# Four gate pairs as 7-product Strassen between the query and the pooling units, attention with one filler unit per block, three pooling groups on GpSimd

## The reference

```
h = RMSNorm(x) * (1 + scale1(c)) + shift1(c)          # from c @ w_ada (1024 x 6144)
u, q, k, v, ga, gb = split(h @ w_in)                  # widths 512, 512, 128, 128, 1024, 1024
A = pool(u) @ w_a      # 4 groups of 128: causal mean over 2, 4, 8, 16 tokens minus token, 128 x 128 map, scale
B = attention(q, k, v) @ w_b     # window 128, 8 heads on 2 kv heads, ALiBi, sinks
x = x + gate1(c) * ((sigmoid(ga) * A + sigmoid(gb) * B) @ w_out)
h2 = RMSNorm(x) * (1 + scale2(c)) + shift2(c)
x = x + gate2(c) * (relu(h2 @ w_up)^2 @ w_down);  y = RMSNorm(x)
```

## Time and profile before

| | |
|---|---|
| median of 3 runs | 1286.92 us (1286.79 to 1288.46) |
| the profiled execution | 1287.11 us, span 1285.4 us |
| TensorE matmul / weight load busy | 1264.3 us (98%) / 1237.8 us (96%) |
| VectorE, ScalarE, GpSimd busy | 826.5 (64%), 557.2 (43%), 191.2 us (15%) |
| moved by DMA | 211.59 MB, mean 165 GB/s |

### The profile page before, as it was taken

One profiled execution on the slowest core, in us unless ns is written; L12 is line 12 of the kernel. 1 busy time (PEld: TensorE's weight loads), 2 busy tenths in 40 slices (PEclk: granted clock), 3 DMA queues, 4 the chain that ended last, 5 costly groups with the idle time before them and its releaser, 6 DMA issues. The chain is left out here.

```text
span 1285.4 us, 24641 instructions
## 1 busy us (share of the span) xinstructions
PE 1264.3 (98%) x10165; PEld 1237.8 (96%) x10165; DVE 826.5 (64%) x1264; ACT 557.2 (43%) x969; POOL 191.2 (15%) x183
## 2 busy tenths in 40 slices
PE   6999999999999999999999999999999999999997
...
PEclk9999999999999999999999999999999999999999
...
GB/s 324 311 313 277 135 67 68 70 90 75 67 68 76 201 150 70 172 119 148 123 115 189 164 162 135 143 166 127 167 333 271 216 196 209 216 248 195 181 126 102
DMA packets 238556, 211.59 MB, mean 165 GB/s; under 512 B 17169, under 2 KB 219797, under 8 KB 233565
## 3 DMA queue, kind: packets, MB, share of 16 engines
...
...
## 5 line engine op out<-in xcount | busy, mean ns | idle before, releaser
L603 PE MATMUL psum<-xh,b_lo 128*128 128x264 f32 x908 | 257.8, 284 | 0.0
L601 PE MATMUL psum<-xh,b_hi 128*128 128x264 f32 x908 | 256.7, 283 | 0.0
L602 PE MATMUL psum<-xl,b_hi 128*128 128x264 f32 x908 | 256.2, 282 | 0.0
L601 PE MATMUL psum<-dh,e_hi 128*128 128x264 f32 x896 | 255.0, 285 | 0.0
L602 PE MATMUL psum<-dl,e_hi 128*128 128x264 f32 x896 | 253.9, 283 | 0.0
L603 PE MATMUL psum<-dh,e_lo 128*128 128x264 f32 x896 | 253.7, 283 | 0.0
L601 PE MATMUL psum<-h_hi,w_hi 128*128 128x384 f32 (+1 forms) x624 | 207.9, 333 | 3.0 <-issue 1.7
L602 PE MATMUL psum<-h_lo,w_hi 128*128 128x384 f32 (+1 forms) x624 | 201.5, 323 | 0.0
L603 PE MATMUL psum<-h_hi,w_lo 128*128 128x384 f32 (+1 forms) x624 | 201.3, 323 | 0.0
L602 PEld LDWEIGHTS psum<-xl,b_hi 128*128 128x128 f32 x908 | 170.5, 188 | 0.0
L601 PEld LDWEIGHTS psum<-xh,b_hi 128*128 128x128 f32 x908 | 170.5, 188 | 0.0
(11 more groups left out here) (320 smaller groups left out, 2359.0 us busy)
## 6 DMA issues: line engine op xcount, KB each, us to landing
...
```

What stands on the lines that cost most here:

```text
L601: mm(out, whi, rhi, start=first, stop=False)
L602: mm(out, whi, rlo, start=False, stop=False)
L603: return mm(out, wlo, rhi, start=False, stop=last)
```

## The change

Four of the eight gate pairs leave the attention blocks. They become 28 Strassen products (`gp`), 7 for each pair, between z units 5 and 6: T1 to T4 of h are made during units 2 to 5 (`tx_dve`, `tx_high`, at the tiles in `TX_DVE`, `TX_ACT`), weights come in blocks of 512 rows (`load_gp`), VectorE adds the products up (`gp_product`) and each half gate goes to DRAM by itself (`keep_gate`). The w_ada products move up to before tile 9, the sample attention to tiles 12 to 20; its inputs load during the last pair. An attention block keeps one filler unit: z unit 9 in the first, then gate units. Scores, parting and weighing of neighbouring blocks interleave otherwise, in other banks. Pooling groups 1 to 3 are computed on GpSimd, in blocks 0 to 3, behind its casts. Elsewhere only semaphore counts shift. Cut to its core, eight columns of indentation less:

```diff
 Z_ROW = (KZ, VZ, 0, 1, 2, 3, 4, 5, 6, 7)
-N_Z, N_G, N_AB, N_O = 10, 16, 8, 16
+PAIRS = 4
+N_GP = 7 * PAIRS
+N_Z, N_G, N_AB, N_O = 10, 2 * (DK - PAIRS), 8, 16
...
+TX = [(x, tok) for x in (T1, T2, T3, T4) for tok in range(2)]
+N_T = len(TX)
+TX_DVE = {0: (("raw", T1, 0),), 1: (("raw", T1, 1),), 2: (("raw", T2, 0),), 3: (("raw", T2, 1),), 4: (("low", T1, 0), ("low", T1, 1)),
+  7: (("low", T2, 0), ("low", T2, 1)), 10: (("raw", T3, 0), ("raw", T3, 1), ("raw", T4, 0), ("raw", T4, 1)),
+  11: (("low", T3, 0), ("low", T3, 1))}
+TX_ACT = {2: ((T1, 0),), 3: ((T1, 1),), 5: ((T2, 0),), 6: ((T2, 1),), 11: ((T3, 0), (T3, 1))}
+def gp_place(j, w):
+    return {"11": 0, "21": 1, "12": 3, "22": 2 + 2 * (j % 2)}[w]
...
+GP_BASE = [16 * sum(gp_place(*r) == k for r in GP_LOADS) for k in range(6)]
+def gp_sum(n):
...
...
-REST_SLOT = (0, 1, 0, 1, 0, 1, 1, 1)
-REST_AT = {1: 0, 3: 1, 5: 2, 7: 3, 9: 4, 12: 5, 15: 6, 18: 7}
+REST_SLOT = (0, 1, 0, 1, 0, 1, 0, 1)
+REST_AT = {0: 1, 2: 2, 3: 3, 5: 4, 6: 5, 8: 6, 9: 7}
...
...
@@ -708,11 +788,17 @@
                     last.then_inc(ready[3 * s + t], 1)
                 if (k, s, t) in ((1, 0, 0), (2, 1, 0), (4, 0, 0)):
                     pair_turn({1: 1, 2: 2, 4: 3}[k])
+                if (k, s, t) == (6, 1, 2):
+                    rest_rows(0)
+                if (k, s, t) == (7, 0, 1):
+                    rest_turn(0)
...
+    for u in range(2, N_Q):
         for t in range(3):
             i = 3 * (u - 2) + t
             if i - 1 in REST_AT:
                 rest_turn(REST_AT[i - 1])
             if i in REST_AT:
                 rest_rows(REST_AT[i])
...
+    for n in range(N_GP):
+        i, bank = n % 7, 2 * (n % 4)
+        wait(pe, free[bank], take(bank, ("gp", n)))
+        if n < 4:
+            wait(pe, free[bank + 1], banks.n[bank + 1])
+        pe.wait_ge(b_lo_done, n + 1)
...
+            for k in range(4):
+                last = mm3(psum[:, bank + tok, 0:HB], gp_hi[n % 3][:, k, :], gp_lo[n % 3][:, k, :], xhi[:, k, :], xlo[:, k, :], k == 0, k == 3)
+        last.then_inc(ready[bank], 1)
+    copied(("gp", N_GP - 4))
+    for u in range(N_Q, N_Z - 1):
+        for t in range(3):
+            i = 3 * (u - 2) + t
...
+            if t == 0:
+                pe.wait_ge(w_lo_done, u + 1)
+            tile(("z", u, t), t, t, u, h_hi, h_lo)
+    copied(("gp", N_GP - 1))
...
     for i in range(BLK):
-        u = W_G + 2 * i
-        turn_values(i)
+        kind, u = FILL[i]
         scores(i)
         pe.wait_ge(w_lo_done, u + 1)
-        tile(("g", u, 0), 0, 0, u, h_hi, h_lo)
-        tile(("g", u, 1), 1, 1, u, h_hi, h_lo)
-        tile(("g", u, 2), 2, 2, u, h_hi, h_lo)
-        turn_probs(i, 0)
+        tile((kind, u, 0), 3 * i % 2, 0, u, h_hi, h_lo)
+        if i:
+            weigh(i - 1)
+        turn_values(i)
+        tile((kind, u, 1), (3 * i + 1) % 2, 1, u, h_hi, h_lo)
         if 1 <= i < 5:
             pool_map(i - 1)
-        pe.wait_ge(w_lo_done, u + 2)
-        if i == BLK - 1:
-            last_gate(i, u + 1)
-            continue
-        tile(("g", u + 1, 0), 0, 0, u + 1, h_hi, h_lo)
-        turn_probs(i, 1)
-        tile(("g", u + 1, 1), 1, 1, u + 1, h_hi, h_lo)
-        weigh(i)
-        tile(("g", u + 1, 2), 2, 2, u + 1, h_hi, h_lo)
-        if i == 5:
+        if i == 6:
             pe.wait_ge(tail_done, 1)
             wait(pe, free[3], take(3, "pool_last"))
             for g in range(NG):
@@ -876,6 +972,12 @@
             for g in range(NG):
                 last = nc.tensor.transpose(psum[0:NB * PAD, 4, g * P:(g + 1) * P], pool_tail[:, g, :], ident[:, :])
             last.then_inc(ready[4], 1)
+        tile((kind, u, 2), 3 * i % 2, 2, u, h_hi, h_lo)
+        turn_probs(i, 0)
+        if i < BLK - 1:
+            turn_probs(i, 1)
+    pe.wait_ge(w_lo_done, W_G + N_G)
+    last_gate(BLK - 1, W_G + N_G - 1)
...
+    def tx_high(x, tok):
+        act.wait_ge(n2_t, TX.index((x, tok)) + 1)
+        if x == T2:
+            for j in range(4, DK):
+                act.wait_ge(xt_saved[j], 16)
+        fn(tx_hi[x, tok][:, :, :], tx_raw[x, tok][:, :, :], ACT.Copy).then_inc(n2_hi, 1)
+    def gp_high(n):
...
+        act.wait_ge(landed_sem, value)
+        there(last_of[4] if n == 0 else last_of[5] if n < 3 else ("gp", n - 3))
+        fn(gp_hi[n % 3][:, :, :], place[:, :, :], ACT.Copy, scale=-1.0 if n % 7 == 6 else 1.0).then_inc(b_hi_done, 1)
...
+    for u in range(2, N_Q):
+        if u + 1 < N_Q:
+            split_hi(u + 1)
+        else:
+            gp_high(0)
...
-            if i == 12:
+            for what in TX_ACT.get(i, ()):
+                tx_high(*what)
+            z_copy(u, t)
+    for n in range(N_GP):
+        j, i = divmod(n, 7)
+        if n == 0:
+            gp_high(1)
+        if n + 2 < N_GP:
+            gp_high(n + 2)
+        if n < 2:
+            tx_high(T4, n)
+        if i < 2:
+            done = there(("gp", n))
...
+            bank, _ = turn["gp", n]
+            fn((gp_m1, gp_m5)[i][:, :, :], psum[:, bank:bank + 2, 0:HB], ACT.Copy).then_inc(done, 1)
+    split_hi(N_Q)
...
-        u = W_G + 2 * i
+        u = FILL[i][1]
         split_hi(u + 1)
+        if u + 1 == W_P:
+            split_hi(W_G)
+        fill_copy(i, 0)
+        exps(i, 0)
+        if i:
+            o_copy(i - 1)
         done = there(("v", i))
         fn(v_tok[:, i % 2, :], psum[:, 7, 0:P], ACT.Copy).then_inc(done, 1)
-        exps(i, 0)
-        gate_copy(i, 0, 0)
         exps(i, 1)
-        gate_copy(i, 0, 1)
-        gate_copy(i, 0, 2)
+        fill_copy(i, 1)
...
+        fill_copy(i, 2)
+    split_hi(W_AB)
...
@@ -1578,6 +1734,7 @@
         if p < 3:
             by_token(2 * p + 3)
     split_lo(2)
+    rest_add(0)
...
+    def tx_dve(what, x, tok):
+        raw = tx_raw[x, tok][:, :, :]
+        if what == "low":
+            dve.wait_ge(n2_hi, TX.index((x, tok)) + 1)
...
+            tt(tx_lo[x, tok][:, :, :], raw, f(tx_hi[x, tok][:, :, :]), ALU.subtract).then_inc(h2_done, 1)
+            return
+        if x == T1:
+            ch.step(tt(scr[tok][:, :, :], f(half_x(h_hi, X12, tok)), f(half_x(h_lo, X12, tok)), ALU.add))
+            ch.step(tt(raw, scr[tok][:, :, :], f(half_x(h_hi, X11, tok)), ALU.subtract))
+            tt(raw, raw, f(half_x(h_lo, X11, tok)), ALU.subtract).then_inc(n2_t, 1)
+        elif x == T2:
+            ch.step(tt(raw, f(half_x(h_hi, X22, tok)), f(half_x(h_lo, X22, tok)), ALU.add))
+            dve.wait_ge(n2_t, TX.index((T1, tok)) + 1)
+            tt(raw, raw, tx_raw[T1, tok][:, :, :], ALU.subtract).then_inc(n2_t, 1)
+        else:
+            dve.wait_ge(n2_t, TX.index((T2, tok)) + 1)
+            y = X11 if x == T3 else X21
+            ch.step(tt(raw, scr[tok][:, :, :], f(half_x(h_hi, y, tok)), ALU.subtract))
+            tt(raw, raw, f(half_x(h_lo, y, tok)), ALU.subtract).then_inc(n2_t, 1)
...
+    def gp_low(n):
+        dve.wait_ge(b_hi_done, n + 1)
+        place, hi, lo = gp_from(n)[0][:, :, :], f(gp_hi[n % 3][:, :, :]), gp_lo[n % 3][:, :, :]
+        if n % 7 == 6:
+            stt(lo, place, -1.0, hi, ALU.mult, ALU.subtract).then_inc(b_lo_done, 1)
+        else:
+            tt(lo, place, hi, ALU.subtract).then_inc(b_lo_done, 1)
+    def gp_product(n):
+        j, i = divmod(n, 7)
+        if i < 2:
+            return
+        done = there(("gp", n))
+        bank, turns = turn["gp", n]
...
+        if i == 2:
+            freed(("gp", n - 2))
+            tt(u, p, m1, ALU.add).then_inc(done, 1)
+            dve.wait_ge(done, turns + 1)
+            freed(("gp", n - 1))
+            wait(dve, g_saved[0], 32 * j)
+            ch.step(tt(c12, u, m5, ALU.add))
+        if i == 3:
+            tt(c12, p, c12, ALU.add).then_inc(done, 1)
+        if i == 4:
+            tt(u, p, u, ALU.add).then_inc(done, 1)
+            dve.wait_ge(done, turns + 1)
+            wait(dve, g_saved[1], 32 * j)
+            tt(c22, u, m5, ALU.add).then_inc(c_done, 1)
+        if i == 5:
+            tt(c11, p, m1, ALU.add).then_inc(done, 1)
+        if i == 6:
+            tt(c21, p, u, ALU.add).then_inc(done, 1)
...
-    for u in range(2, N_Z):
+    dve.wait_ge(h_done, DK)
+    dve.wait_ge(hs_done, DK // 2)
+    for u in range(2, N_Q):
         for t in range(3):
             i = 3 * (u - 2) + t
             if i - 1 in REST_AT:
                 rest_add(REST_AT[i - 1])
-            if i == 12:
+            if t == 0 and u + 1 < N_Q:
+                split_lo(u + 1)
+            if t == 0 and u + 1 == N_Q:
+                gp_low(0)
+                gp_add(1)
+                gp_add(2)
+            for what in TX_DVE.get(i, ()):
+                tx_dve(*what)
+    for n in range(N_GP):
+        if n == 0:
+            gp_low(1)
+        else:
+            gp_product(n - 1)
+        if n + 2 < N_GP:
+            gp_low(n + 2)
+        if n + 3 < N_GP and gp_sum(n + 3):
+            gp_add(n + 3)
+        if n < 2:
+            tx_dve("low", T4, n)
+    gp_product(N_GP - 1)
+    split_lo(N_Q)
...
+            if i in S_NORM:
```

(147 more changed lines are left out.)

249 lines of the change are left out of this document (158 added, 91 removed).

## The result

The changed kernel takes **1302.29 us** (median of 4 runs, 1301.51 to 1306.33) against 1287.03; the ratio is 1.0123, 95% interval 1.0101 to 1.0145, so it is slower by 15.3 us. The forecast was 1290.6 with a range of 1281 to 1300: the side was right, the size was not, and the time lies 2.3 us above the range.

The account below looks back on a forecast made before the run. TensorE's work, plus any waits put into it, was taken to bound the kernel: span 1285.4 - 12.2 + 9.4 + 3.0 + 0.5 + 3.0 = 1289.1 us, forecast 1290.6 against the median, range 1281 to 1300.

Parts of the forecast that it names:

- Products: Four gate pairs as seven products each, 120.5 ns per matmul: 3.04 us saved per pair, 12.2 us in all.
- The w_ada loads: Eight 2 MB blocks, needed earlier while DMA engines are full, stall TensorE 9.4 us; bounds 5.8 to 12.9.
- Rest 1: w_ada block needed before tile 0: lands at 65.8 us, stalling TensorE 2.75 us.
- Rest 3: w_ada block needed before tile 3: queued behind other loads, lands at 84.0 us, stall 2.5 us.
- Rest 6: w_ada block needed before tile 8: queued behind gate blocks, leaves at 105.2 us, stall 3.9 us.
- T3 and T4: VectorE derives them at tile 10, 13.4 us against TensorE's 10.4, so product 1 is late by 3.0 us.
- Behind the last product: VectorE drains it, then splits unit 6, while TensorE has 1.5 us of turning: 0.5 us wait.
- Attention: Blocks with one filler: GpSimd's pooling sums and VectorE stop one another, 3 us reach TensorE; bounds 0 and 14.
- (a): Rival: w_ada loads stay mostly hidden, DMA engines moving 400 GB/s in the mix, a gain, say 1283 us; chance 0.25.
- (b): Rival: GpSimd and VectorE starve one another in attention blocks 1 to 3, up to 14 us: 1302; chance 0.14.
- (c): Rival: gate products miss the feed-forward pace, at 125 ns per matmul the saving falls by 3 us: 1294; chance 0.09.
- rival (d): New TensorE stalls drop the clock to 1.2 GHz for 4 us of work behind each: 1300 us; chance 0.05.

Follow-up runs that it names:

- experiment 4: Changed kernel with one late w_ada load issued ahead of the four gate blocks and T2's halves made at later tiles: 1296.29 us.
- experiment 7: Changed kernel with pooling groups 1 to 3 back on VectorE, one behind the splits of each of blocks 0 to 2: 1310.19 us.
- experiment 1: Changed kernel with idle transposes of a constant tile on TensorE ahead of four waits: 1294.86 us.
- experiment 2: Kernel before with three added TensorE waits: 1306.92 us (four tiles of zeros each), 1292.01 (one tile), 1302.14 (four tiles, waits filled with idle turns).

## Why the prediction was wrong

- **What bounds the kernel**: right. All that was lost, but for 1.3 us, shows as a wait of TensorE or as its clock.
- **Products**: -12.2 predicted, -11.7 measured (121.2 ns for each matmul and not 120.5; the window of the earlier trace rows also counts matmuls that were already under way at 1100 us, and by starts the feed-forward part has 120.8).
- **The w_ada loads**: 9.4 predicted, 11.4 measured, within the bounds of 5.8 to 12.9. Rest 1: 2.75 and 1.6; it landed at 65.97 us for 65.8, but TensorE came to it 1.2 us late from the low clock of the start. Rest 3: 2.5 and 4.6; it landed 10.4 us after its issue at 76.3, and the engines moved 299 and 338 GB/s from 66 to 78 us, below the 344 taken. Rest 6: 3.9 and 5.2; the mechanism, the gate blocks held by T2's high half, was the right one, and ScalarE's rows and experiment 4 show it, only rest 6 left at 108.3 and not 105.2 and shared the engines with rest 7, issued with it (12.1 us to landing, not 8.9). Rest 7: 0.3 and 0.
- **T3 and T4**: 3.0 and 3.1 (the terms as written add up to 13.3 and not 13.4).
- **Behind the last product**: 0.5 and 0.6.
- **Attention**: 3 predicted, 1.4 measured. Both engines did hold one another, in the sizes named: a one-line maximum of VectorE beside a GpSimd sum took 1.66 us, and a GpSimd sum beside a VectorE subtraction 2.86 where most of its kind take 1.89.

```profile
304.77 1.66 DVE L1951 TENSOR_TENSOR mx<-mx,sink_p 128x4 f32<-128x4 f32 x1
...
306.98 2.86 POOL L2390 TENSOR_TENSOR win_b<-win_a 128x1020 f32<-128x1020 f32 x1
```

  But the cover of 14 us took most of it, and experiment 7 shows that the move pays: 7.9 us, part of it the clock's. What the Trainium skill says of the shared interfaces ("GPSIMD Engine Reference", section Key points) agrees with these rows; its advice of VectorE for elementwise work did not decide here, because VectorE had no time left.
- **Not foreseen**: 1.1 us at the sample weighing (VectorE's pooling group ahead of it), 0.6 at the first down product, 1.5 at the first branch product. That last one is a queue: the gate pair is fetched only when the last gate's store has landed, 439.13 - 434.05 = 5.1 us after its issue where it was 2.7 before.
- **The clock, the step that failed.** The waits sum to 19.7 where the forecast had 15.9, and 1287 - 11.7 + 19.7 = 1295 is inside the range; 1294.9 is what the kernel took with the clock held up (experiment 1). That the single terms are this near is in part luck: attention was put too high by 1.6, and 3.2 came from places not foreseen. What put the time outside is that the forecast priced a wait at its length alone, because "the granted clock is 1.00 in all stretches with matmuls", and gave rival (d) 0.05. But the kernel before has no wait of over 0.8 us between 32 and 1270 us, so its row spoke only for a TensorE that never stops, and only for one execution: the clock at the start fell in others (experiment 2). The runs showed in its place that the low clock costs about 7 us of the median. Rival (d)'s price, 2 to 4 us for each wait and 1300 in all, was about right, although no row then bore its 4 us at the lower level: 2.5 each in experiment 2, 1.5 to 3.1 in the windows above. Its chance was far too low once the forecast's own sum had four waits of 2.5 to 3.9 us: in the traces on record five of nine waits of 2.3 to 3.7 us had a fall (last section). The Trainium skill's warning of gaps between bursts ("TensorE: Matmul & The Clock Gate", section Why this matters for your kernels) agrees with the falls at all waits of 4.15 us and more. The clock also fell behind waits of 1.1 and 1.9 us, which are shorter than the gaps that it warns of; there the measurement decides.
- **Rivals**: (a) fell with the loads; (b) did not occur; (c) added 0.5 us; (d) decided. The side, slower, was no luck: with the clock held up the kernel is slower too (1.0061).
